# Past pages four sequences abreast, log-weights written over the softplus, scores half a period ahead, and a moved store

## The reference

```python
z = jnp.einsum('bqhd,bkhd->bhqk', qb, kb).astype(jnp.float32) * scale + bias
log_1m = jnp.where(mask, jax.nn.log_sigmoid(-z), 0.0)
log_w = jax.nn.log_sigmoid(z) + lax.cumsum(log_1m, axis=3, reverse=True) - log_1m
w = jnp.where(mask, jnp.exp(log_w), 0.0)
outs.append(jnp.einsum('bhqk,bkhd->bqhd', w.astype(vb.dtype), vb))
```

## Time and profile before

| | us |
|---|---|
| median of 3 runs (lowest to highest) | 2439.23 (2437.92 to 2440.74) |
| the profiled execution, whole | 2440.66 |
| its span, first to last instruction | 2439.0 |
| PE busy | 2391.9 (98%) |
| DVE busy | 1242.9 (51%) |
| ACT busy | 996.7 (41%) |
| POOL busy | 114.9 (5%) |

### The profile page before, as it was taken

How to read it: one execution, slowest core, us unless ns; L and a number is a source line. 1 busy time by engine, 2 the same in 40 slices (tenths; PEclk the granted TensorE clock), 3 DMA queues, 4 the chain that set the end, 5 groups by cost and what they waited for, 6 DMA issues and landing times.

```text
span 2439.0 us, 43786 instructions
## 1 busy us (share of the span) xinstructions
PE 2391.9 (98%) x18794; PEld 2184.2 (90%) x18794; DVE 1242.9 (51%) x1725; ACT 996.7 (41%) x1399; POOL 114.9 (5%) x232
## 2 busy tenths in 40 slices
PE   6999999999999999999999999999999999999998
PEld 5999999965599999999999999887777999999998
DVE  4533336755576332357533346745555658633245
ACT  4522234635456222346522245523322546522243
POOL 0000000121100000000000000011222100000000
PEclk8999999999999999999999999999999999999999
DMA  8555455775536644565755345654555456643254
GB/s 282 178 165 173 129 183 178 257 217 126 191 115 213 199 160 135 178 210 176 242 160 169 117 156 184 189 165 156 166 171 168 131 172 184 190 142 92 86 178 154
DMA packets 122658, 417.09 MB, mean 171 GB/s; under 512 B 23386, under 2 KB 27610, under 8 KB 122210
## 3 DMA queue, kind: packets, MB, share of 16 engines
q1 hardware_dynamic: 89538, 302.08, 39.2%
q10 hardware_dynamic: 17568, 61.87, 7.5%
q0 software_dynamic: 15360, 50.34, 6.4%
HBM read 390.84 MB, written 23.41 MB: 170 GB/s over the span
## 4 chain that ended last, share of the span: by engine, by line
PE 88%; DVE 5%; ACT 3%; DMA 2%; issue 2%; SPq 0%; POOLq 0%; POOL 0%; ACTq 0%; DVEq 0%
PE PS L2008 71%; PE PS L1403 3%; PE PS L1942 3%; PE PS L1972 2%; PE PS L1333 1%; DVE WL L2292 1%; ACT WH L2120 1%; DMA AFIRST<-in_w_ada 1%; PE PS L769 1%; PE PS L1287 1%; PE PS L1318 1%; PE PS L1328 1%; PE PS L1299 1%; ACT Y L2169 1%; PE PS L772 1%
## 5 line engine op out<-in xcount | busy, mean ns | idle before, releaser
L2292 DVE TENSOR_TENSOR WL<-RAW,WH 128x1024 fp32r<-128x1024 f32 (+1 forms) x478 | 633.1, 1325 | 677.2 <-ACT WH L2120 676.5
L2008 PE MATMUL PS<-HH,WH 128*128 128x260 f32 x3432 | 799.6, 286 | 3.0 <-DVE QKVS L1097 1.0
L2008 PE MATMUL PS<-HH,WL 128*128 128x260 f32 x3432 | 786.0, 282 | 0.0
L2008 PE MATMUL PS<-HL,WH 128*128 128x260 f32 x3368 | 769.6, 283 | 0.0
L2120 ACT ACTIVATE WH<-RAW 128x1024 fp32r<-128x1024 f32 (+1 forms) x478 | 542.4, 1135 | 402.7 <-PE PS L2008 275.3
L2008 PEld LDWEIGHTS PS<-HH,WH 128*128 128x128 f32 x3432 | 569.2, 188 | 35.3 <-issue 26.6
L2008 PEld LDWEIGHTS PS<-HH,WL 128*128 128x128 f32 x3432 | 569.3, 188 | 0.0
L2008 PEld LDWEIGHTS PS<-HL,WH 128*128 128x128 f32 x3368 | 557.5, 188 | 0.6 <-issue 0.2
L2008 PE MATMUL PS<-GH,WH 128*128 128x260 f32 x1408 | 386.3, 284 | 0.1
L2008 PE MATMUL PS<-GL,WH 128*128 128x260 f32 x1408 | 384.2, 283 | 0.0
L2008 PE MATMUL PS<-GH,WL 128*128 128x260 f32 x1408 | 383.5, 283 | 0.0
(11 more groups left out here) (338 smaller groups left out, 2313.7 us busy)
## 6 DMA issues: line engine op xcount, KB each, us to landing
RAW<-in_w_in SPq DMA_DIRECT2D x236, 512.0 KB, 3.6
RAW<-in_w_out SPq DMA_DIRECT2D x120, 704.0 KB, 4.0
AW<-in_w_ada ACTq DMA_DIRECT2D x114, 512.0 KB, 4.5
RAW<-in_w_odd SPq DMA_DIRECT2D x60, 512.0 KB, 3.6
RAW<-in_w_odout SPq DMA_DIRECT2D x30, 512.0 KB, 3.7
RAW<-in_w_even SPq DMA_DIRECT2D x28, 512.0 KB, 4.2
KV<-in_v_pages POOLq DMA_DIRECT2D x32, 256.0 KB, 4.9
SR<-in_ret_past POOLq DMA_DIRECT2D x32, 256.0 KB, 4.0
```

Source lines behind the costliest of these rows:

```text
L2008: last = nc.tensor.matmul(ps[:, x, 0:HT], w[:, k * P:(k + 1) * P], src[k0 + k][:, x, :], start=(begin and t == 0), stop=(end and t == 2))
L2292: nc.vector.tensor_tensor(low_, RAW[:, from_:from_ + w], high_.bitcast(F32), ALU.subtract).then_inc(lo_done, 1)
```

## The change

What it does, part by part:

- `scores_past(q)` takes two pages each of four sequences (pages 2 (q mod 2) and the next, sequences 4 (q // 2) to 4 (q // 2) + 3) where it took four pages of two, so its products use all four column groups: 16 products of 256 columns for 8 of 512. `values_past(q)` likewise: 8 products of 512 columns over four groups. POOL loads the pages in that order.
- `scores_past(0)` and `(1)` both stand at (21, 1), `(2)` at (25, 0), `(3)` at (26, 0). DVE's clearing of their bank moves from i = 21 to i = 19.
- `log_weights` writes into the softplus's tile `SP` and no longer into `ZS`; the exponentials are taken there in place. `ZS` of a pair is then free once its log-weights are made, and `scored` waits for these (`lw_done`) where it waited for `w_done`.
- The scores of a pair start half a period earlier: blocks 0 and 1 of pair t + 2 stand in the second half of period t, blocks 2 and 3 at the start of period t + 1. `values(t - 1)` stands after `sums(2t, 1)`, and on DVE `sized` comes before the later log-weights.
- The store `pool_n` moves on SP from its place behind the keys to the place behind the `AW` loads of head 1; `pool_p` goes out first, and DVE waits for it alone (`pool_out`).

The store of 4096 pieces now stands between the `AW` loads of head 1 and those of head 2, in the same queue. The diff, cut:

```diff
         def biased_to(t, j):
-            return 8 if (t, j) == (1, 0) else 10 * t - 4 if j == 0 else 10 * t - 2 + 2 * j
+            return 4 * t + 4 if t < 1 else 10 * t + 2 * j
+
+        def bank_free_at(t, j):
+
+            return biased_to(t, j - 1) if j else 8 if t == 1 else biased_to(t - 1, 3)
         def sized_to(t, e):
...
-                    for dst, src in ((k_t[:, 0:4 * SEQ], KP[:]), (k_t[:, 4 * SEQ:4 * SEQ + 32], QKVS[:, 4:8, :]),
-                                     (pool_p, UP[:, :, SEQ + 1:SEQ + 16]), (pool_n, US[:, :, :, 1:16])):
+                    sp.dma_start(pool_p, UP[:, :, SEQ + 1:SEQ + 16]).then_inc(pool_out, 16)
+                    for dst, src in ((k_t[:, 0:4 * SEQ], KP[:]), (k_t[:, 4 * SEQ:4 * SEQ + 32], QKVS[:, 4:8, :])):
...
                         for c in ADA_LOADS["head", h]:
                             sp.wait_ge(ada_mm, c + 1)
                             sp.dma_start(AW[:, c % 2, :], w_ada[c]).then_inc(ada_in[c % 2], 16)
+                        if h == 1:
+                            sp.dma_start(pool_n, US[:, :, :, 1:16]).then_inc(late_out, 16)
                 load("evout", i)
         def even_pe(pe, products, ada_step, stats):
...
                 bufs = (0, 1) if q % 2 == 0 else (2, 3)
                 for n in bufs:
                     pe.wait_ge(kv_in[n], 64 * (q // 2 + 1))
+                keys = slice(2 * P * (q % 2), 2 * P * (q % 2) + 2 * P)
                 for t in range(4):
-                    for b, n in zip((2 * q, 2 * q + 1), bufs):
-                        c = 96 * t + 24 * (b % 4) + 8 * (b // 4)
-                        last = nc.tensor.matmul(PS[2][32 * (b % 4):32 * (b % 4) + 16, 0, :], QBM[:, c:c + 16],
-                                                PAGE[n][:, :, t * P:(t + 1) * P], start=(b < 4 and t == 0),
-                                                stop=(b >= 4 and t == 3), tile_position=(0, 32 * (b % 4)))
+                    for g in range(4):
+                        c = 96 * t + 24 * g + 8 * (q // 2)
+                        last = nc.tensor.matmul(PS[2][32 * g:32 * g + 16, 0, keys], QBM[:, c:c + 16],
+                                                PAGE[bufs[g // 2]][:, 2 * (g % 2):2 * (g % 2) + 2, t * P:(t + 1) * P],
+                                                start=(q == 0 and t == 0), stop=(q == 3 and t == 3),
+                                                tile_position=(0, 32 * g))
                 last.then_inc(kv_used, 1)
             def values_past(q):
...
-                for p in range(PAGES):
-                    for n in range(2):
-                        b = 2 * q + n
-                        c = p * P + 32 * (b % 4) + 8 * (b // 4)
-                        last = nc.tensor.matmul(PS[3][32 * (b % 4):32 * (b % 4) + 8, 1, :], ZW[:, c:c + 8],
-                                                PAGE[n][:, p, :], start=(p == 0), stop=(p == PAGES - 1),
-                                                tile_position=(0, 32 * (b % 4)))
+                for k in range(2):
+                    p = 2 * (q % 2) + k
+                    for g in range(4):
+                        c = p * P + 32 * g + 8 * (q // 2)
+                        last = nc.tensor.matmul(PS[3][32 * g:32 * g + 8, 1, :], ZW[:, c:c + 8],
+                                                PAGE[g // 2][:, 2 * (g % 2) + k, :], start=(p == 0),
+                                                stop=(p == PAGES - 1), tile_position=(0, 32 * g))
...
-                if half == 1 and i in (22, 23, 24, 25):
-                    scores_past(i - 22)
+                if (i, half) == (21, 1):
+                    scores_past(0)
+                    scores_past(1)
+                if half == 0 and i in (25, 26):
+                    scores_past(i - 23)
...
-                if t == PAIRS:
+                if t >= PAIRS:
...
-                pe.wait_ge(z_dve, biased_to(t, j))
+                pe.wait_ge(z_dve, bank_free_at(t, j))
...
             sums_past()
             scores_of_one()
+            scores(1, 0)
             ada_step("start", 0)
+            scores(1, 1)
             for t in range(PAIRS):
-                scores(t + 1, 0)
+                scores(t + 1, 2)
                 sums(2 * t, 0)
-                scores(t + 1, 1)
+                scores(t + 1, 3)
+                sums(2 * t, 1)
                 if t:
                     values(t - 1)
-                sums(2 * t, 1)
-                scores(t + 1, 2)
                 sums(2 * t, 2)
                 if t == 2:
                     gather(0)
-                scores(t + 1, 3)
                 sums(2 * t, 3)
                 if t < 3:
                     values_past(t)
                 ada_step("head", 2 * t)
-                for i in range(4):
+                sums(2 * t + 1, 0)
+                scores(t + 2, 0)
+                sums(2 * t + 1, 1)
+                scores(t + 2, 1)
+                for i in (2, 3):
                     sums(2 * t + 1, i)
                 if t == 3:
                     values_past(3)
...
-                nc.scalar.activation(SP[h % 4], ZS[h % 4], ACT.Exp).then_inc(w_done, 1)
+                nc.scalar.activation(SP[h % 4], SP[h % 4], ACT.Exp).then_inc(w_done, 1)
...
-                z = ZS[h % 4][:, OFF[i]:OFF[i] + LEN[i]]
-                nc.vector.tensor_tensor(z, z, PS[1][:, i % 2, 0:LEN[i]], ALU.subtract).then_inc(lw_done, 1)
+                at_ = slice(OFF[i], OFF[i] + LEN[i])
+                nc.vector.tensor_tensor(SP[h % 4][:, at_], ZS[h % 4][:, at_], PS[1][:, i % 2, 0:LEN[i]],
+                                        ALU.subtract).then_inc(lw_done, 1)
...
             def scored(t, j):
-                if t == PAIRS:
+                if t >= PAIRS:
                     return
-                if j == 0:
-                    after(dve, w_done, 2 * t - 2)
-                    if t == 1:
-                        dve.wait_ge(out_done, 96)
+                if (t, j) == (1, 0):
+                    dve.wait_ge(pool_out, 16)
                 for e in range(2):
+                    after(dve, lw_done, 4 * (2 * t - 4 + e) + j + 1 if t > 1 else 0)
                     dve.wait_ge(z_done, 8 * t + 2 * j + e + 1)
                     biased(2 * t + e, j, PS[0][:, e, 0:LEN[j]])
...
+                if i == 19:
+                    dve.wait_ge(mod_ready, 4)
+                    nc.vector.memset(PS[2][:, 0, :], 0.0).then_inc(z_zero, 1)
...
-                    dve.wait_ge(mod_ready, 4)
-                    nc.vector.memset(PS[2][:, 0, :], 0.0).then_inc(z_zero, 1)
...
             dve.wait_ge(unit_done, POS["evin"] + len(EV))
             nc.vector.tensor_tensor(ZN[:, 0, :], ZN[:, 0, :], PS[2][:, 0, :], ALU.subtract).then_inc(zn_dve, 1)
             scored_one()
+            scored(1, 0)
+            scored(1, 1)
             nc.vector.tensor_copy(VSR[0:NS, :], PS[3][0:NS, 1, :]).then_inc(vs_ok, 1)
             dve.wait_ge(vs_ok, 1)
             nc.vector.memset(PS[3][:, 1, :], 0.0).then_inc(pz_ok, 1)
             for t in range(PAIRS):
                 if t == 2:
                     copy_past(0)
-                scored(t + 1, 0)
+                scored(t + 1, 2)
                 log_weights(2 * t, 0)
-                scored(t + 1, 1)
+                scored(t + 1, 3)
+                log_weights(2 * t, 1)
+                sized(t + 1, 0)
+                if t == 2:
+                    copy_turned(0)
+                log_weights(2 * t, 2)
+                sized(t + 1, 1)
+                log_weights(2 * t, 3)
                 if t:
                     low(t - 1)
-                log_weights(2 * t, 1)
-                scored(t + 1, 2)
-                scored(t + 1, 3)
-                if t == 2:
-                    copy_turned(0)
-                sized(t + 1, 0)
-                log_weights(2 * t, 2)
-                log_weights(2 * t, 3)
-                sized(t + 1, 1)
                 if t == 0:
                     softplus(1)
                 ada_evac("head", 2 * t)
                 for i in range(2):
                     log_weights(2 * t + 1, i)
+                    scored(t + 2, i)
                 if t < 3:
                     softplus(2 * t + 2)
                 for i in range(2, 4):
...
-            def pages(src, b, n):
...
-                for p in range(PAGES):
-                    at_ = b * PAGES + p
-                    row = pool.value_load(PT[0:1, at_:at_ + 1], min_val=0, max_val=PHYS - 1)
-                    pool.dma_start(PAGE[n][:, p, :], src[bass.ds(row, 1)].rearrange(
-                        "o p n -> (o p) n")).then_inc(kv_in[n], 16)
+            def pages(src, q, n, buf):
...
+                for e in range(2):
+                    for k in range(2):
+                        at_ = (4 * (q // 2) + 2 * n + e) * PAGES + 2 * (q % 2) + k
+                        row = pool.value_load(PT[0:1, at_:at_ + 1], min_val=0, max_val=PHYS - 1)
+                        pool.dma_start(PAGE[buf][:, 2 * e + k, :], src[bass.ds(row, 1)].rearrange(
```

(24 more changed lines are left out.)

## The result

The changed kernel takes 2444.22 us (median of 14 runs, 2441.73 to 2448.98), the kernel before 2439.74 beside it (14 runs): ratio 1.0021, 95% interval 1.0014 to 1.0028. It is slower by 4.5 us where 4 us less were forecast, and outside the range of 2430.5 to 2441.5. The profiled execution took 2444.87 us (span 2442.9), against 2440.66 before: 4.2 more. (One of the 12 executions with seven idle matmuls, further on, ran at a granted clock of 0.739 and took 2955 us; its median is of the other eleven.)

What follows compares the result with a forecast made beforehand. PE, busy 98% of the span, was taken as the bound, so shorter PE work had to win. Terms -6.6 - 1.9 - 6.0 + 3.2 + 1.6 + 1.5 + 4.1 = -4.1 us gave 2435.1 us, range 2430.5 to 2441.5.

Steps and rivals of the forecast that it cites:

- past keys: Four calls of `scores_past`: each falls from 3.55 us to 1.9 with four column groups abreast, -6.6 us in sum.
- wait for key pages: PE's 1.88 us wait for key pages goes, as call 3 comes later and its pages are asked for earlier: -1.9 us.
- past values, at full clock: Four calls of `values_past`: each falls from 3.4 us to 1.9 with four groups, -6.0 us in sum.
- first pooling product's cover: At `pooled(0)`: past scores no longer fill the time until DVE's last difference, so PE waits, +3.2 us (0 to 3.5).
- head 0's scores' cover: At (26, 0): `first_scores(1)` follows `scores_past(3)` at once and waits for DVE's first bias, +1.6 us (0 to 1.8).
- start of the heads: At `scores(1, 0)` and the blocks behind it, PE waits for score banks and DVE's biases: +1.5 us (0.5 to 2).
- later periods: Log-weights cost the same and the wait before `scores(3, 1)` stays under another name: 0 us (-1.5 to +2).
- moved store, wait: At `values_past(1)`: `pool_n` delays value pages, a wait of 3.6, and `AW` loads, 0.5 more: +4.1 us (0 to 12).
- The slower rival: At `values_past(1)`: the store holds value pages longer than before, a wait of 11; 2443.0 us in sum, chance 0.09.
- signs of being wrong: Wait ahead of second past values under 1 us or over 8, past-key call over 2.5, or softplus idling each period turn.
- the lost covers cost nothing: Rival: DVE is earlier than thought, so +3.2 at `pooled(0)` and +1.6 at head 0's scores vanish; 2430.3 us, chance 0.08.
- No overlap of four groups: Rival: the four column groups don't run beside each other, past keys and values cost as before; 2447.7 us, chance 0.06.

Runs made afterwards that it cites:

- seven idle matmuls: Changed kernel plus seven matmuls of 512 columns whose results nobody uses, ahead of the second past values: 2442.67 us against 2440.41 for the kernel before.

## Why the prediction was wrong

Term by term, in us, from the profiled execution:

| term of the sum | forecast | measured |
|---|---|---|
| past keys | -6.6 | -7.0 (4 x 3.55 less 1.8) |
| wait for key pages | -1.9 | -1.9 |
| past values, at full clock | -6.0 | -6.8 (4 x 3.4 less 1.7) |
| first pooling product's cover | +3.2 | +3.1 |
| head 0's scores' cover | +1.6 | +1.5 |
| start of the heads | +1.5 | +1.75, and 0.56 more for head 1's softplus |
| later periods | 0 | +1.0 (waits of 0.8 + 1.1 + 0.96 for 1.49 + 0.3) |
| moved store, wait | +4.1 | +6.0 |
| half clock behind that wait | not in the sum | +2.5 |
| half clock behind a lost cover (1.7) and at the heads' start (1.6) | not in the sum | +3.3 |
| sum | -4.1 | +4.0 |

The terms that were read from rows of this kernel hold within about 1 us each; store and half clock aside they come to 7.8 us faster. The stage itself, from the end of step 21 to the heads' end on PE, takes 153.7 us (507.92 to 661.60) where it took 150.1 (509.91 to 660.04): 3.6 more, so the terms miss it by 0.4. The rest of the 4.2 lies outside the stage, about 2 won ahead of it and 2.3 lost behind it, and is scatter (behind the heads the twelve traces of this case take 1778.7 to 1781.3 us); that the sum comes so near to the whole is chance. What failed:

*The moved store.* The place, the mechanism and the moment were right (value pages beside 60-byte pieces, a wait ahead of the second past values), the size was not. The step took the pages to land 12.6 us after the last issue; they landed 609.42 - 593.75 = 15.7 after it. PE came 0.7 later than forecast against the issues, so 3.6 became 3.6 + 3.1 - 0.7 = 6.0. PE waits for the last of eight pages, so of the earlier trace rows the maximum, 15.7, was the row to take and not the middle; four of those eight were issued before the store's pieces moved, at 543, where here all were issued with the store or behind it. The further 0.5 for ada loads was not seen. The runs with the whole, half and no store there (6.04, 0.39, none) show the cause. The slower rival came nearest in its number, 2443.0, but by a wait of 11 us where 6.0 was measured; that nearness is luck.

*A wait was priced at its own length.* Behind every one of the five waits for pages of 5.1 to 8.7 us in these traces the clock was granted at 0.50 for some microseconds, and the same instructions took up to twice as long (3.37 us for 1.72). The forecast rested on "at the full granted clock" of the earlier trace rows, which held for a PE that hardly ever stood; the change itself took that away. This missing term is 5.8 us. Without its two rows the measured sum would be -1.8, still faster and inside the range, so it is this step that turned the sign. None of the signs of being wrong that the prediction names came (the wait is between 1 and 8, a past-key call took 1.74, only head 1's softplus made PE wait): none of them looks at the clock. The slower rival was set to begin where pages land later than 614: with 2.5 us of half clock behind the wait and 3.3 elsewhere, it begins far sooner.

*The rival "the lost covers cost nothing"* is refuted by the rows; mended, together with head 1's softplus, they gave 7.4 us, half clock included. *No overlap of four groups* is refuted at 1.74.

## What to carry to other kernels

Before a store of short pieces is moved off one load, look at which loads are issued in the microseconds behind its new place, and whether the old collision is still there once the other edits are made. Price a new wait of TensorE by its length and by the instructions behind it at half the clock. Edits ahead of an outstanding transfer gained little here until that transfer was early: mend the transfer first, then the covers.

## What the runs showed that was not expected

The clock falls behind short waits too, but not every time: behind the wait of 1.53 us at 549 it fell in three of the six executions that have it (the changed kernel and both with idle matmuls; not with the store back, with half the store, or with the heads' old start), behind the 3.13 us at the first pooling product in three of the same six, others than these in part, and at the heads' start, where PE waits 0.2 to 1.2 us at a time, in four of the seven with the new order. What decides there stays open; the executions without these waits show no fall at these places. That part of the price (3.3 us in the profiled execution) is therefore one execution's, and runs may have less or more of it.

The store's time from issue to landing hardly depended on its place: 23.0 to 24.6 us at the new one, 20.9 to 21.7 behind the keys, and half of it 12.5 to 13.1.
